# Splitting the last stage of a decoder-step kernel into column halves, with its square root on GpSimd and the last expert's weights loaded in parts

## What is computed

```
x = x + w1 * y_expert1 + w2 * y_expert2              (experts: silu(h @ w_gate) * (h @ w_up) @ w_down)
gate = sigmoid(rmsnorm(x, g_ple) @ w_ple_gate)
x = x + (p @ w_ple) * gate
y = rmsnorm(x, g_final)        rmsnorm(x, g) = x * rsqrt(mean(x * x) + 1e-6) * g
```

## Time and profile before

| | |
|---|---|
| median of 3 executions | 1148.91 us (1146.29 to 1150.71) |
| profiled execution: time / span | 1153.33 us / 1151.6 us |
| TensorE matmul busy | 928.9 us (81% of the span) |
| VectorE, ScalarE, GpSimd busy | 354.6, 172.0, 303.6 us |
| share of the chain that ended last | TensorE 45%, DMA 33%, VectorE 12% |
| last stage, from the first load of expert rows to the end | 1059.87 to 1151.6 us |

### The profile page before, as it was taken

The page is one execution under the profiler, slowest core; times in us unless marked ns, Lnnn a source line. Parts: engine busy times, 40 slices in busy tenths (PEclk is TensorE's granted clock), DMA queues, the critical chain, the costliest instruction groups (busy, mean ns, idle before and its releaser), DMA issues.

```text
span 1151.6 us, 11801 instructions
## 1 busy us (share of the span) xinstructions
PE 928.9 (81%) x4354; PEld 491.3 (43%) x4354; DVE 354.6 (31%) x831; ACT 172.0 (15%) x333; POOL 303.6 (26%) x310
## 2 busy tenths in 40 slices
PE   3999899899579777966987797778777888884795
PEld 2678667666464333533333333333333333331342
DVE  6044455566765122255000000000000000001775
ACT  2010232232200000021111101110111011110321
POOL 6238877877201222001111101110111111000000
PEclk9999989899768779888889988898899878988898
DMA  9126754654421897660699999999999999997301
GB/s 302 29 85 219 269 197 161 214 183 146 174 101 53 304 396 325 252 260 14 242 408 411 399 407 401 404 413 399 416 414 406 401 405 407 424 406 284 110 20 55
DMA packets 52232, 314.31 MB, mean 273 GB/s; under 512 B 10934, under 2 KB 23798, under 8 KB 31192
## 3 DMA queue, kind: packets, MB, share of 16 engines
q1 hardware_dynamic: 29264, 230.30, 50.0%
q0 software_dynamic: 14512, 76.17, 18.1%
q10 hardware_dynamic: 8416, 7.30, 2.0%
HBM read 307.18 MB, written 14.82 MB: 280 GB/s over the span
## 4 chain that ended last, share of the span: by engine, by line
PE 45%; DMA 33%; DVE 12%; issue 4%; ACT 3%; POOL 1%; SPq 1%; ACTq 0%; DVEq 0%; POOLq 0%
DMA arena<-in_w_up 28%; PE psum L1432 13%; PE psum L1060 7%; PE psum L1134 6%; PE psum L1286 4%; DMA arena<-in_cache_v,indices 4%; PE psum L1197 2%; PE psum L1147 1%; PE psum L1534 1%; PE psum L1447 1%; DVE arena L1560 1%; DVE arena L2047 1%; PE psum L1390 1%; PE psum L1173 1%; PE psum L1048 1%
## 5 line engine op out<-in xcount | busy, mean ns | idle before, releaser
L1432 PE MATMUL psum<-arena 128*64 128x512 f32 x1024 | 273.3, 694 | 86.4 <-DMA arena<-in_w_up 86.4
L1432 PEld LDWEIGHTS psum<-arena 128*64 128x64 f32 x1024 | 92.3, 159 | 243.4 <-issue 243.1
L632 POOL TENSOR_TENSOR arena<-arena 128x2048 f32<-128x2048 f32 x32 | 145.1, 4535 | 33.6 <-ACTq L768 33.1
L2017 DVE TENSOR_TENSOR arena<-arena,psum 64x512 f32<-64x512 f32 x32 | 22.1, 691 | 389.1 <-ACT arena L968 389.1
L1447 PE MATMUL psum<-arena 128*64 128x512 f32 x512 | 115.9, 592 | 0.5 <-DVE arena L2021 0.5
L661 POOL COPY indices<-row_list 128x1 int32 (+1 forms) x32 | 5.7, 179 | 375.3 <-ACT arena L974 375.3
L1134 PE MATMUL psum<-arena 128*128 128x260 f32 x320 | 87.0, 419 | 8.1 <-ACT arena L823 6.4
L1060 PE MATMUL psum<-arena 128*128 128x260 f32 x384 | 85.7, 386 | 0.7 <-ACT arena L753 0.7
L1597 DVE TENSOR_REDUCE arena<-arena 128x32 f32<-128x2048 f32 (+1 forms) x32 | 72.9, 2281 | 23.8 <-POOL arena L632 21.9
L1060 PEld LDWEIGHTS psum<-arena 128*128 128x128 f32 x384 | 73.7, 192 | 12.6 <-ACT arena L753 1.2
L1134 PEld LDWEIGHTS psum<-arena 128*128 128x128 f32 x320 | 61.7, 203 | 31.9 <-ACT arena L823 11.5
(11 more groups left out here) (309 smaller groups left out, 917.3 us busy)
## 6 DMA issues: line engine op xcount, KB each, us to landing
arena<-in_w_gate SPq DMA_DIRECT2D x32, 2048.0 KB, 18.3
arena<-in_w_up SPq DMA_DIRECT2D x32, 2048.0 KB, 22.7
...
```

What stands on the lines that cost most here:

```text
L632: pool.tensor_tensor(r, r, q_rep, ALU.mult).then_inc(kmul, 1)
L1432: last = mm(bank(s)[m * SLOTS:(m + 1) * SLOTS, :], hgT[s][:, k, :], w_gu[s][m][:, k, :], start=(k == 0), stop=(k == DC - 1))
```

## The change

1. The last expert's gate and up weights are loaded as eight transfers of 512 KB in place of two of 2 MB, gate and up in turn, by pairs of the eight 128-row blocks; `gate_up` of that expert waits for each pair when it comes to it.
2. For the last six scatters GpSimd copies the row numbers before it waits for ScalarE's copy.
3. All five tiles have a buffer for their expert rows, and all loads are issued at once.
4. TensorE turns the raw x. The root scales the sigmoid's input instead, as a per-row factor of the ScalarE instruction.
5. Both roots are taken by GpSimd: a multiply-add and a power of -0.5, one element per row.
6. Everything behind a gate matmul goes by halves of 512 columns: each half of the matmuls signals, and has its own sigmoid, its own multiply and add, and its own sum of squares. GpSimd adds up the two sums. Of the output, VectorE scales the second half; the first half is multiplied by g_final before the root is known, and ScalarE multiplies the root in.
7. The transposes of tile i+1 stand behind the fourth matmul of tile i, the samples' matmuls are in two parts around the transposes of tile 1, and VectorE's order is changed to suit.

SP and GpSimd:

```
             sp.wait_ge(gu_full, NE - 2)
-            load_expert(NE - 1, 1)
+            for n in range(LAST_PARTS):
+                ks = slice(n * DC // LAST_PARTS, (n + 1) * DC // LAST_PARTS)
+                for m, w in enumerate((wg, wu)):
+                    rows = w[NE - 1:NE].rearrange("o (p k) f -> p (o k) f", k=DC)
+                    sp.dma_start(w_gu[1][m][:, ks, :], rows[:, ks, :]).then_inc(gu_last[n], 16)
             for e in (NE - 2, NE - 1):
                 sp.wait_ge(y_full, e - 1)
                 load_down(e, e % 2)
...
             sp.wait_ge(moe_done, 1)
             for n, t in enumerate(LAST):
                 w = tile_width(t)
-                if n >= 2:
-                    sp.wait_ge(x2_ready, n - 1)
                 rows = moe_dram[4 * t * P:4 * (t * P + w), :].rearrange("(p k) d -> p (k d)", k=4)
-                sp.dma_start(pairs_in[n % 2][0:w, :], rows).then_inc(pairs_ready[n % 2], 16)
+                sp.dma_start(pairs_in[n][0:w, :], rows).then_inc(pairs_ready[n], 16)
             for n, t in enumerate(LAST):
                 w = tile_width(t)
-                sp.wait_ge(y_final, n + 1)
+                sp.wait_ge(y_final, 2 * n + 2)
                 dst = y_prompt[0, t * P:(t + 1) * P, :] if t < QT else y_sample.rearrange("b l d -> (b l) d")
                 sp.dma_start(dst, y_buf[n % 2][0:w, :]).then_inc(y_stored[n % 2], 16)
...
-            def scatter(e, s):
-                step(pool.tensor_copy(row_ix[s][:, 0:1], row_list[:, bass.ds(e, 1)]))
+            def scatter(e, s, copied=False):
+                if not copied:
+                    step(pool.tensor_copy(row_ix[s][:, 0:1], row_list[:, bass.ds(e, 1)]))
                 return pool.indirect_dma_start(moe_dram, bass.IndirectOffsetOnAxis(ap=row_ix[s][:, 0:1], axis=0),
                                                y_rows[s], None, bounds_check=2 * PAIRS - 1, oob_is_err=False)
...
                 if exists(i, c - 2):
+                    s = (c - 2) % RING
+                    if last:
+                        pool.wait_ge(y_out[s], loads(i, c - 2 - RING, RING))
+                        step(pool.tensor_copy(row_ix[s][:, 0:1], row_list[:, c - 2:c - 1]))
                     pool.wait_ge(y_copied, num(i, c - 1))
                     if not isinstance(i, int):
                         alone(pool)
-                    scatter(num(i, c - 2), (c - 2) % RING).then_inc(y_out[(c - 2) % RING], 16)
+                    scatter(num(i, c - 2), s, copied=last).then_inc(y_out[s], 16)
...
+            step = Steps(pool, pool_post)
+            minus_half = stats[:, 47:48]
+            step(pool.memset(minus_half, -0.5))
+            def root_x2(n):
+                t = LAST[n]
+                w = tile_width(t)
+                pool.wait_ge(x2_ms, n + 1)
+                step(pool.tensor_scalar(root2(t), stats[0:w, 32 + t:33 + t], 1.0 / D, EPS, ALU.mult, ALU.add))
+                pool.tensor_tensor(root2(t), root2(t), minus_half[0:w, :], ALU.pow).then_inc(r2_ready, 1)
+            def root_x4(n, h):
+                t = LAST[n]
+                w = tile_width(t)
+                pool.wait_ge(x4_ms, 2 * n + h + 1)
+                if h == 0:
+                    step(pool.tensor_scalar(root4(t), square4(t, 0), 1.0 / D, EPS, ALU.mult, ALU.add))
+                    return
+                step(pool.tensor_scalar(root4(t), square4(t, 1), 1.0 / D, root4(t), ALU.mult, ALU.add))
+                pool.tensor_tensor(root4(t), root4(t), minus_half[0:w, :], ALU.pow).then_inc(r4_ready, 1)
+            root_x2(0)
+            root_x2(1)
+            for n in range(TILES):
+                root_x4(n, 0)
+                if n + 2 < TILES:
+                    root_x2(n + 2)
+                root_x4(n, 1)
```

ScalarE (`finish_gate` is gone; `root4` and `square4` are like `root2`, one column of `stats` each):

```
+        def root2(t):
+            return stats[0:tile_width(t), 37 + t:38 + t]
+        def root4(t):
+            return stats[0:tile_width(t), 42 + t:43 + t]
+        def square4(t, h):
+            return stats[0:tile_width(t), 48 + t:49 + t] if h == 0 else stats[0:tile_width(t), t:t + 1]
...
+                if n:
+                    act.wait_ge(x2_ms, n)
                 act.activation(junk2[0:w, :], x[0:w, t, :], ACT.Square, accum_out=stats[0:w, 32 + t:33 + t]).then_inc(x2_ms, 1)
+            def gate_half(n, h):
+                t = LAST[n]
+                w = tile_width(t)
+                act.wait_ge(pg_full, 2 * n + h + 1)
+                act.wait_ge(r2_ready, n + 1)
+                gate = ple_gate[n % 2][0:w, half_of(h)]
+                src = bank(2 * (n % 2) + h)[0:w, :]
+                if t == QT:
+                    src = gate
+                    if h == 0:
+                        copy_parts(act, parts_g, bank(2 * (n % 2)))
+                        act.wait_ge(parts_summed, 1)
+                act.activation(gate, src, ACT.Sigmoid, scale=root2(t)).then_inc(pg_sig, 1)
+            def square_x4(n, h):
+                t = LAST[n]
+                w = tile_width(t)
+                act.wait_ge(x4_ready, 2 * n + h + 1)
+                if n:
+                    act.wait_ge(x4_ms, 2 * n + h - 1)
+                act.activation(junk4[0:w, half_of(h)], x[0:w, t, half_of(h)], ACT.Square, accum_out=square4(t, h)).then_inc(x4_ms, 1)
+            def scale_y(n):
+                t = LAST[n]
+                y = y_buf[n % 2][0:tile_width(t), half_of(0)]
+                act.wait_ge(xg_ready, n + 1)
+                act.wait_ge(r4_ready, n + 1)
+                act.activation(y, y, ACT.Copy, scale=root4(t)).then_inc(y_final, 1)
             square_x2(0)
             square_x2(1)
             for n in range(TILES):
+                gate_half(n, 0)
+                square_x4(n, 0)
                 if n + 2 < TILES:
                     square_x2(n + 2)
-                finish_gate(act, n)
+                gate_half(n, 1)
+                square_x4(n, 1)
+                scale_y(n)
```

TensorE:

```
-            def gate_up(s, signal):
+            def gate_up(s, signal, parts=None):
                 for k in range(DC):
+                    if parts is not None and k % (DC // LAST_PARTS) == 0:
...
-                    pe.wait_ge(gu_in[c % 2][m], loads(i, c, 2))
-                gate_up(c % 2, gu_full)
+                if last:
+                    gate_up(c % 2, gu_full, gu_last)
+                else:
+                    for m in range(2):
+                        pe.wait_ge(gu_in[c % 2][m], loads(i, c, 2))
+                    gate_up(c % 2, gu_full)
                 if exists(i, c - 1):
                     down_step(i, c - 1)
                 pe.wait_ge(act_ready, num(i, c + 1))
...
-                w = tile_width(LAST[i])
-                pe.wait_ge(x3_ready, i + 1)
+                t = LAST[i]
+                w = tile_width(t)
+                pe.wait_ge(x2_ready, i + 1)
                 for s in range(2):
                     if 2 * i + s >= 2:
                         pe.wait_ge(xT_ready, 2 * i + s - 1)
                     for c in range(4):
                         k = 4 * s + c
-                        last = tr(bank(4 + s)[:, c * P:c * P + w], xn[i % 2][0:w, k * P:(k + 1) * P], ident[0:w, 0:w])
+                        last = tr(bank(4 + s)[:, c * P:c * P + w], x[0:w, t, k * P:(k + 1) * P], ident[0:w, 0:w])
                     last.then_inc(xT_full, 1)
             transpose_x(0)
             pe.wait_ge(xT_ready, 2)
-            sample_sums(mm, bank(0), xT[0], w_gate_ple).then_inc(pg_full, 1)
+            sample_sums(mm, bank(0), xT[0], w_gate_ple, range(DC // 2))
             transpose_x(1)
+            sample_sums(mm, bank(0), xT[0], w_gate_ple, range(DC // 2, DC)).then_inc(pg_full, 2)
             for i in range(1, TILES):
-                pe.wait_ge(xT_ready, 2 * i + 2)
-                if i >= 2:
-                    pe.wait_ge(pg_sig, i - 1)
                 for n in range(2):
+                    if i >= 2:
+                        pe.wait_ge(pg_sig, 2 * (i - 2) + n + 1)
                     for k in range(DC):
-                        if (n, k) == (1, DC // 2) and i + 1 < TILES:
+                        if n == 0 and k % 4 == 0:
+                            pe.wait_ge(xT_ready, 2 * i + k // 4 + 1)
+                        if (n, k) == (0, DC // 2) and i + 1 < TILES:
                             transpose_x(i + 1)
                         last = mm(bank(2 * (i % 2) + n), xT[i % 2][:, k, :], w_gate_ple[:, k, n * BANK:(n + 1) * BANK],
                                   start=(k == 0), stop=(k == DC - 1))
-                last.then_inc(pg_full, 1)
+                    last.then_inc(pg_full, 1)
```

VectorE:

```
-            def add_experts(n):
+            def add_experts(n, choices=(0, 1)):
                 t = LAST[n]
                 w = tile_width(t)
-                dve.wait_ge(pairs_ready[n % 2], 16 * (n // 2 + 1))
-                for c in range(2):
-                    step(v.scalar_tensor_tensor(out=x[0:w, t, :], in0=pairs_in[n % 2][0:w, c * D:(c + 1) * D],
+                dve.wait_ge(pairs_ready[n], 16)
+                for c in choices:
```

(51 more changed lines are left out.)

67 lines of the change are left out of this document (21 added, 46 removed).

## The result

Changed kernel: median 1140.37 us (7 runs, 1138.4 to 1144.82); kernel before, beside it: 1150.71 us (7 runs, 1146.29 to 1154.05). Ratio 0.992, 95% interval 0.9898 to 0.9942: 0.8% faster, some 10 us where 13.8 were forecast. (The forecast of 1135.1 us was made against a median of 1148.91, so 1.8 of the 5.3 us between it and 1140.37 lie in the base.) A second set of runs gave 0.9927 (0.9899 to 0.9955). The profiled execution took 1142.64 us, with a span of 1140.8.

What follows compares the result with a forecast made beforehand. Weight loads were taken to pace the expert stage, TensorE's gate matmuls the last stage. Gains of 2.3 + 5.7 + 1.9 + 3.9 = 13.8 us took the median from 1148.9 to 1135.1 us, range 1131.5 to 1137 (chance 0.55).

Steps and rivals of the forecast that it cites:

- 1. The last expert: Last expert's path from weight loads to scatter: 2.3 us earlier, between 0.8 and 3.3.
- TensorE's 1.3: Last expert: weights in parts let the last down matmuls start when their own weights land, 1.3 us earlier.
- The gap's 2.0: Last scatter: row numbers copied before the wait cut the gap behind ScalarE's copy from 2.54 to 0.5 us.
- The scatter's 1.0: Last scatter: issued while gate weights still arrive, it takes 1.0 us longer to land, between 0 and 2.
- Rival A: Last expert gives nothing: the unnamed 2.24 us stay, the landing grows by what was saved; 1137.4 us, chance 0.14.
- 2. The start: Start of the last stage: first gate matmul of tile 1 comes 5.7 us earlier, between 3.0 and 6.3.
- 3. The body: Gate matmuls and transposes of the last stage: 58.7 us instead of 60.7, 1.9 us gained, between 0.4 and 2.2.
- rival B: Last stage: other engines do not keep pace, through a slow power or handovers, with stalls; 1138 to 1141 us, chance 0.15.
- 4. The tail: Last matmul to end of last output operation: 4.5 us instead of 8.4, 3.9 gained, between 2.1 and 4.2.
- No cost: Last stage: small root operations, loads of tiles 2 to 4 and the sigmoid's table load add no time.
- Rival C: Last stage: TensorE's clock stays at half, one whole tile costing 13.9 us more; 1149 us, chance 0.03.
- D: Whole change: gives half of what is forecast, through rivals A, B and a late clock together; 1141 us, chance 0.08.

Runs made afterwards that it cites:

- base_after: The changed kernel itself, unaltered, run once more on the chip of later runs; 1140.7 us, 0.992 of the kernel before.
- e16: Changed kernel, but the second half of the last stage's gate weights and the final scale load behind the first expert rows; 1139.94 us, ratio 0.9905.
- e6: Changed kernel, but the last expert's gate and up weights in whole loads as before; 1142.06 us (one execution).
- e18: Changed kernel, last root on VectorE, last expert's transposes ahead of expert 30's down matmuls, last gate-weight quarter and final scale loaded behind row loads; 1137.18 us, 0.9896.
- e4: Changed kernel with all roots of the last stage on VectorE, none on GpSimd; 1144.69 us.
- e10: Changed kernel, but TensorE's transposes of each tile also wait for that tile's root; 1151.5 us (one execution).
- e11: Changed kernel, but ScalarE starts a tile's first half only when both halves of its gate matmuls are done; 1151.27 us.

## Why the prediction was right in its direction and 5 us off

**What bounds.** Right: TensorE in the body, the stage around it in four stretches.

**1. The last expert, 2.3 us: wrong, it is about nothing.** The trace gives 1.1 us, and base_after, the same code, −0.5. All three terms of 1.3 + 2.0 − 1.0 failed. In the changed kernel's trace they measured 0.4, 0.2 and +0.5.

*TensorE's 1.3.* I let the last down matmuls start when their own weights land. These landed at 1045.2, but the matmuls started at 1046.88, because expert 30's down matmuls stand ahead of them, waited for their weights until 1040.25, and took 5.35 us at the fallen clock. The prediction named that landing (1041.2) and did not follow it through TensorE's list. That the clock would fall I had not seen.

*The gap's 2.0.* The copy of the row numbers was worth 0.18 us (from ScalarE's copy to the transfer 2.36 against 2.54), and the 2.24 stayed.

*The scatter's 1.0, "between 0 and 2".* It was a price where the runs show a tie: for a scatter that starts up to 4 us ahead of the gate weights' landing, the bytes queued ahead set when it lands, and what is saved on TensorE, ScalarE or GpSimd ahead of it is lost again. The 13 profiles show it by last down matmuls that move against the queue while the row load does not, e16 by an edit of the queue that moved the row load alone. I had the earlier trace rows, and read it as a price list instead of asking which transfers set the end. I also misread it: its median of 7.0 is over transfers that include loads of expert rows. The row of the six scatters alone is

```profile
DMA to landing us min/median/max: 4.4/7.9/9.1
```

Rival A had the outcome of this term, zero, and half of the reason: the 2.24 us stay, and the landing grows by what was saved. In base_after, where the clock did not fall, the row load came no earlier (46.0 us), so the fall seems to have cost nothing; no run was made to show that.

**2. The start, 5.7 us: right.** 5.1 in this trace, 5.5 to 6.2 in the others with the same start. The first half of the sample matmuls took 3.60 us at the half clock (3.4 forecast), the second 2.15 in this trace and 1.90 in others (1.7). VectorE waited 0.23 us for tile 1's rows, as worked out from the earlier trace rows. The point at which the clock rose did vary: the eight transposes between the two halves took 1.97 us here, 1.50 in e6 and 1.09 in e18, and the granted clock rose 6.0 us behind the start of the samples' matmuls here, 3.5 in e18. That it varies agrees with the rule of the Trainium skill ("TensorE: Matmul & The Clock Gate", Part 1) that the prediction weighed; these 2.5 us are more than its ±500 ns.

**3. The body, 1.9 us: right in kind, 2.8 measured.** No joint of 0.5 exists: the records follow one another without a gap, so 57.9, not 58.7. The stall feared at tile 3's transposes did not come, and the power took 0.55 us; rival B falls. e4, e10 and e11 show how near it was: each takes one relief away, and the body goes to 64 to 66 us.

**4. The tail, 3.9 us: 3.5.** The tail is 4.9 for 4.5. The root on GpSimd cost 0.94 us for 0.85; its two steps 0.26 and 0.55. The factor two of the Trainium skill ("GPSIMD Engine Reference", Key points), by which VectorE's 0.16 would become 0.3, agrees with the first step, 0.26; the power is slower than it. In the tail VectorE rests. In the body the same kind of multiply-add takes 1.18 us twice, while VectorE adds expert rows, and 0.19 in the last two tiles, where it does not; it costs nothing there, and no run separates the two:

```profile
1088.65 1.18 POOL L732 TENSOR_SCALAR arena<-arena 128x1 f32<-128x1 f32 x1 [4.20 <-ACT arena L1068]
...
1113.45 0.19 POOL L732 TENSOR_SCALAR arena<-arena 128x1 f32<-128x1 f32 x1 [5.53 <-ACT arena L1068]
```

The rest of the tail is in half-width operations, 0.70 each instead of 0.68 and 0.59 for ScalarE's.

**No cost: the term that was missing.** Nothing was charged for moving work to an engine that had been idle at the end. Its closing drain, 5.5 us long and hidden at 1059.9 before, became the end of the program: 1.9 us. The row stood in the trace of before, and I had not looked at what ends the program behind the last output.

Together: 13.8 − 2.3 (last expert) − 1.9 (drain) − 0.6 + 0.9 − 0.4 (start, body, tail) = 9.5 us, which is what the traces give from the first row load on, 91.7 to 82.2, and near the 10.3 us of the medians. Rival C falls: the clock was 1.00 through the body. The measured 1140.37 us lies by the times of rivals B (1138 to 1141) and D (1141), but by luck: B's stalls did not come, and D asks for A, B and a late clock together, of which only A came; neither has the drain. The low end of the range is 1131.0 by its own sum (1132.9 less 1.9), not 1131.5; nothing hangs on it.
